# Weighing the exponentials of a sparse attention inside their transposes: one diagonal product in place of a scaling and a transpose

## The chip, the cores and the metric

One Trainium2 chip, one of its cores. The time is the device time of one execution in microseconds, as the median of a kernel's runs. The core's engines are TensorE (PE in the profile, its weight loads apart as PEld), VectorE (DVE), ScalarE (ACT), GpSimd (POOL) and SyncE (SP), each with an instruction queue of its own; they wait for one another through semaphores.

## What is computed

A network of three layers runs on 256 tokens of width 1024: a first layer (latent attention beside a recurrence, then experts), an even layer and an odd layer, each of the last two with a feed-forward part. The change lies in the odd layer's attention, which for 8 pairs of heads has a compressed branch, a "selected" branch and a window branch. With 256 tokens all blocks are selected and the window covers everything, so both of the latter are causal attentions over all keys, each with its own keys and values, and each weighed by a gate of its own per token and head:

```
s = jnp.einsum('bqghd,bgqnld->bqghnl', qb, kg).astype(jnp.float32) * scale
p = safe_softmax(s.reshape(B, C_Q_BLOCK, C_GROUPS, C_HPG, top_n * SEL_BLOCK), m_slc)
o_slc = jnp.einsum('bqghnl,bgqnld->bqghd', p.astype(vg.dtype), vg)
...
s = jnp.einsum('bqghd,bsgd->bqghs', qb, kwb).astype(jnp.float32) * scale
p = safe_softmax(s, m_win)
o_win = jnp.einsum('bqghs,bsgd->bqghd', p.astype(vwb.dtype), vwb)
g = qslice(gates, i, C_Q_BLOCK)
return g[..., 0:1] * o_cmp + g[..., 1:2] * o_slc + g[..., 2:3] * o_win
```

So each row of exponentials is multiplied by gate / sum before it meets the values.

## The kernel before

The kernel is a sequence of stages with a barrier between them. The function of the change, `sparse_attention`, is one stage; before it `odd_in` makes queries, keys and values, after it `out_ffn` multiplies by the output matrix and runs the feed-forward part. Each stage has hand-written programs for each engine, and the order of the work on an engine is the order of its code; there is no scheduler.

`sparse_attention` runs over 16 units (`units`). Unit u is a pair of heads n and a branch b, `n, b = divmod(u, 2)`; i counts the two heads of the pair. The 256 query tokens are two tiles of 128 (t); by causality tile 0 sees 128 keys and tile 1 sees 256 (`SPAN`), so a head has 384 columns (`NCOL`) of exponentials, in three blocks of 128x128.

A unit goes through these steps, by the names in the code:

- `score(u)` (TensorE, L3596 and L3601): mask and scores into `pS`, signal `scored`.
- `smallest(u)` (VectorE, L3511): the row extremes `low_max`, signal `least`.
- `exps(u)` (ScalarE, L3472): four exponentials into `E`, with row sums into `den`, signal `exped`. From u = 2 on it first waits until unit u-2 has been turned (`probs_turned`), since `E` has two buffers.
- `weigh(u)` (VectorE, L3519 to L3525): gate over sum into `part`, then the four pieces of `E` are multiplied in place, signal `weighed`.
- `turn(u)` (TensorE, L3613): six transposes of 128x128 from `E` into `pT`, signal `probs_turned`. It waits for `weighed`, and for the copies of the unit before, as `pT` has one buffer.
- `left(u)` and `right(u)` (VectorE L3532, ScalarE L3481): copies of `pT` into `ET`.
- `add_values(u)` (TensorE, L3626; for b = 1 also the compressed branch, L3634): products with the values into `pO`; after every second unit `high(n)` (ScalarE, L3485) and `rest(n)` (VectorE, L3536) take the result out as two f16 parts, `mixT`.

The engines' programs interleave units. In iteration u, TensorE does `score(u+2)`, `turn(u)`, `add_values(u-1)`; ScalarE does `exps(u+2)`, in odd iterations `high`, then `right(u)`; VectorE does `smallest(u+2)`, `weigh(u+1)`, `left(u)`, and in odd iterations `rest`. TensorE also does the 16 compressed scores (L3643) before iteration 0 and four transposes for them (L3658) in iteration 2. `Link` makes VectorE wait for its own previous result.

Of the kernel before, what the change touches and what calls it, by code (L numbers as in the profile page):

```python
# [9 lines left out]
ALU = mybir.AluOpType  # L10
# [7 lines left out]
P = 128  # L18
SEQ = 256
TT = SEQ // P  # L20
# [13 lines left out]
SPAN = [(0, 0, P), (1, P, SEQ)]  # L34
# [1689 lines left out]
def first_mix(nc, con, m, out, low, shifted, x, wt, w, ring, views, slots, expert, h, scratch, keep, start):  # L1724
# [9 lines left out]
    with ExitStack() as ctx:  # L1734
# [3 lines left out]
        probs = turned4[:].rearrange("p u n -> p (u n)")  # L1738
        E = probs[:, 0:4 * NCOL].rearrange("p (s i n) -> p s i n", s=2, i=2)
        ET = probs[:, 4 * NCOL:8 * NCOL].rearrange("p (s i n) -> p s i n", s=2, i=2)  # L1740
        low_max = sb("low_max", [P, 2, TT, 2])
# [59 lines left out]
        with Stage(nc, "rw", RW_NAMES + TAIL_NAMES + ["few_" + n for n in FEW_NAMES] + ["moe_" + n for n in MOE_NAMES]) as sems:  # L1801
# [33 lines left out]
            with nc.Block(no_gpsimd_drain=True) as block:  # L1835
# [62 lines left out]
                def _(pe):  # L1898
# [131 lines left out]
                    def turn_probs(u):  # L2030
# [5 lines left out]
                        for i in range(2):  # L2036
                            for n in range(3):
                                ins = T.transpose(pB[:, P_BANK[i], n * P:(n + 1) * P], E[:, u % 2, i, n * P:(n + 1) * P],
                                                  con["identity"])
# [187 lines left out]
                def _(act):  # L2227
                    copy = lambda o, i, scale=1.0: nc.scalar.activation(o, i, ACT.Copy, scale=scale)

                    def exps_of(u):  # L2230
# [5 lines left out]
                        for i in range(2):  # L2236
                            for t, c0, nk in SPAN:
                                ins = nc.scalar.activation(E[:, at, i, c0:c0 + nk], scores(u)[:, i, c0:c0 + nk], ACT.Exp,
                                                           bias=low_max[:, at, t, i:i + 1], scale=m.nrq[:, 0, t, 2 * u + i:2 * u + i + 1],
# [732 lines left out]
def even_attention(nc, con, y, e, low, outT, start):  # L2972

    units = 8
    with ExitStack() as ctx:
# [3 lines left out]
        part = sb("part", [P, 2, 2, TT])  # L2979
        E = sb("E", [P, 2, 2, NCOL])  # L2980
        ET = sb("ET", [P, 2, 2, NCOL])
        st = sb("st", [P, 3, 8])
# [444 lines left out]
def sparse_attention(nc, con, y, o, low, outT, start):  # L3427
# [4 lines left out]
    with ExitStack() as ctx:  # L3432
        sb = lambda n, s, d=F32: ctx.enter_context(nc.sbuf_tensor(f"nsa_{n}", s, d))
# [2 lines left out]
        den = sb("den", [P, 2, 2, TT])  # L3436
        part = sb("part", [P, 2, 2, TT])
        E = sb("E", [P, 2, 2, NCOL])
        ET = sb("ET", [P, 2, 2, NCOL])
        cS = sb("cS", [P, 2, TT, PAIRS, CMP_KEYS])  # L3440
        c_max = sb("c_max", [P, n_cmp])
# [4 lines left out]
        pT = ctx.enter_context(nc.psum_tensor("nsa_pT", [P, 2, 512], F32))  # L3446
# [5 lines left out]
        with Stage(nc, "nsa", ["scored", "least", "exped", "weighed", "probs_turned",  # L3452
# [4 lines left out]
            with nc.Block(no_gpsimd_drain=True) as block:  # L3457
# [44 lines left out]
                @block.vector  # L3502
                def _(dve):
                    link = Link(dve, vlink)

                    def smallest(u):
                        dve.wait_ge(scored, u + 1)
                        if u >= 2:
                            dve.wait_ge(exped, u - 1)
                        for t, c0, nk in SPAN:  # L3510
                            ins = nc.vector.tensor_reduce(low_max[:, u % 2, :, t], pS[:, u % 2, :, c0:c0 + nk], AX_X,  # L3511
                                                          ALU.min)
                        ins.then_inc(least, 1)

                    def weigh(u):
                        dve.wait_ge(exped, u + 1)
                        n, b = divmod(u, 2)
                        at = u % 2
                        link(nc.vector.tensor_tensor(part[:, at], den[:, at], gate[:, b + 1, 2 * n:2 * n + 2, :],  # L3519
                                                     ALU.mult))  # L3520
                        link(nc.vector.reciprocal(part[:, at], part[:, at]))
                        for i in range(2):
                            for t, c0, nk in SPAN:
                                into = E[:, at, i, c0:c0 + nk]
                                ins = nc.vector.tensor_scalar(into, into, part[:, at, i, t:t + 1], None, ALU.mult)  # L3525
                        ins.then_inc(weighed, 1)

                    def left(u):
                        dve.wait_ge(probs_turned, u + 1)
                        if u >= 2:  # L3530
                            dve.wait_ge(summed, u - 1)
                        nc.vector.tensor_copy(ET[:, u % 2, 0, :], pT[:, 0, 0:NCOL]).then_inc(probs_left, 1)  # L3532

                    def rest(n):
                        dve.wait_ge(high_out, n + 1)
                        nc.vector.tensor_tensor(outT[1][:, n, :], pO[:, n % 2, 0:SEQ], outT[0][:, n, :],  # L3536
                                                ALU.subtract).then_inc(low_out, 1)

                    over = lambda v: v.unsqueeze(2).broadcast_to([P, n_cmp, CMP_KEYS])
                    flat = cS[:].rearrange("p i t n k -> p (i t n) k")  # L3540

                    def compressed_scores():
                        dve.wait_ge(c_scored, 1)
                        for i in range(2):
                            mask = con["cmp_mask"].rearrange("p (t k) -> p t k", t=TT).unsqueeze(2)\
                                .broadcast_to([P, TT, PAIRS, CMP_KEYS])
                            ins = nc.vector.tensor_tensor(
                                cS[:, i], pT[:, 0, :].rearrange("p (t n i k) -> p i t n k", t=TT, i=2, k=CMP_KEYS)[:, i], mask,
                                ALU.add)
                            link(ins)  # L3550
                        dve.sem_inc(c_masked, 1)
                        link(nc.vector.tensor_reduce(c_max[:], flat, AX_X, ALU.min))
                        nc.vector.tensor_tensor(flat, flat, over(c_max[:]), ALU.subtract).then_inc(c_less, 1)

                    def compressed_weights():
                        dve.wait_ge(c_exped, 1)
                        link(nc.vector.tensor_reduce(c_den[:], flat, AX_X, ALU.add))
                        as_heads = c_den[:].rearrange("p (i t n) -> p i t n", i=2, t=TT)
                        link(nc.vector.tensor_tensor(c_part[:], as_heads, gate_cmp, ALU.mult))
                        link(nc.vector.reciprocal(c_part[:], c_part[:]))  # L3560
                        nc.vector.tensor_tensor(flat, flat, over(c_part[:].rearrange("p i t n -> p (i t n)")),
                                                ALU.mult).then_inc(c_weighed, 1)

                    dve.wait_ge(gate_exps, 1)
                    link(nc.vector.tensor_scalar(gates[:], gates[:], 1.0, None, ALU.add))
                    smallest(0)
                    smallest(1)
                    weigh(0)
                    for u in range(units):
                        if u == 0:  # L3570
                            compressed_scores()
                        if u + 2 < units:
                            smallest(u + 2)
                        if u == 2:
                            dve.wait_ge(c_turned, 1)
                            nc.vector.tensor_copy(cT[:].rearrange("p i s -> p (i s)"), pO[:, 1, :]).then_inc(c_out, 1)
                        if u + 1 < units:
                            weigh(u + 1)
                        left(u)
                        if u == 1:  # L3580
                            compressed_weights()
                        if u >= 3 and u % 2:
                            rest((u - 3) // 2)
                    rest(PAIRS - 1)

                @block.tensor
                def _(pe):
                    ident = con["identity"]
# [17 lines left out]
                    def turn(u):  # L3606
                        pe.wait_ge(weighed, u + 1)
                        if u > 0:
                            pe.wait_ge(probs_left, u)
                            pe.wait_ge(probs_right, u)  # L3610
                        for i in range(2):
                            for k, (t, kb, at) in enumerate(blocks):
                                ins = nc.tensor.transpose(pT[:, i, k * P:(k + 1) * P], E[:, u % 2, i, at:at + P], ident)  # L3613
                        ins.then_inc(probs_turned, 1)

                    def add_values(u):
# [23 lines left out]
                    for n in range(PAIRS):  # L3640
                        for t in range(TT):
                            at = (t * PAIRS + n) * 2 * CMP_KEYS
                            ins = nc.tensor.matmul(pT[:, 0, at:at + 2 * CMP_KEYS], qT[:, n, t * P:(t + 1) * P],  # L3643
                                                   kcT[:, n // per_group].rearrange("p i k -> p (i k)"), start=True, stop=True,
                                                   skip_group_check=True)
                    ins.then_inc(c_scored, 1)
                    for u in range(units):
# [5 lines left out]
                        if u == 2:  # L3653
                            pe.wait_ge(c_weighed, 1)
                            for i in range(2):
                                for t in range(TT):
                                    at = i * SEQ + t * P
                                    ins = nc.tensor.transpose(pO[:, 1, at:at + P], cS[:, i, t].rearrange("p n k -> p (n k)"), ident)  # L3658
# [126 lines left out]
```

## Time and profile before

| | before |
|---|---|
| median of 3 runs | 1140.2 us (1139.49 to 1145.4) |
| profiled execution, span from first to last instruction | 1135.1 us |
| TensorE busy | 998.4 us (88%) |
| VectorE busy | 590.4 us (52%) |
| ScalarE busy | 486.3 us (43%) |
| `sparse_attention`, first score to last result | 853.3 to 921.0 us |

The profile gives no total of its own for the profiled execution: its span of 1135.1 us is 5.1 us less than the median of the runs, and changes of the span are set against it. In the timeline, "idle before" is in brackets with the instruction that ended the wait; several instructions of one kind are one row with their count, and the time of such a row is from the first's start to the last's end. An f32 product can have more records in the trace than the program has instructions; the counts of both are given where this matters.

### The profile page before, as it was taken

To read this page: it belongs to the slowest core of one execution; us is meant where nothing else is said; L and a number is where in the kernel's file an instruction comes from. 1 tells how busy PE (TensorE), PEld (TensorE's weight loads), DVE (VectorE), ACT (ScalarE), POOL (GpSimd) and SP (SyncE) were. 2 spreads that over 40 slices of the span, in tenths; PEclk is the share of its full clock that TensorE was granted. 3 is DMA by queue.
4 is the path that set the end of the run, shared out by engine and by line. 5 is a ranking of instruction groups with operands and counts; after the bars stand their busy time and mean duration, and the time that the engine had idled before them with its cause. 6 is when DMAs were issued, how large, how long until landed. Compare 5 with 4: busy or idle time off the path is not lost. (4 is left out here: it accounts for less than half of the span.)

```text
span 1135.1 us, 20168 instructions
## 1 busy us (share of the span) xinstructions
PE 998.4 (88%) x8497; PEld 710.3 (63%) x8499; DVE 590.4 (52%) x950; ACT 486.3 (43%) x795; POOL 101.3 (9%) x111
## 2 busy tenths in 40 slices
PE   6998899799666677998799999997998879999996
PEld 5675787455333344886547777775885536777773
DVE  5566589421000004688666555435667865555543
ACT  5456452310000004545556455524545656645532
POOL 3410360000000001033000000002040000000000
PEclk9899899799888898998889999998998999999999
DMA  9822005999999996452094755525422046666520
GB/s 273 247 90 82 2 3 226 422 409 420 421 421 421 421 411 195 155 177 76 1 329 133 243 193 184 183 105 153 149 82 75 1 174 216 223 222 204 188 89 37
DMA packets 108324, 228.56 MB, mean 201 GB/s; under 512 B 7145, under 2 KB 86043, under 8 KB 93659
## 3 DMA queue, kind: packets, MB, share of 16 engines
q1 hardware_dynamic: 105275, 219.38, 53.2%
q0 software_dynamic: 2976, 8.14, 2.5%
q8 instruction: 53, 0.87, 0.3%
q14 instruction: 20, 0.16, 0.0%
HBM read 224.63 MB, written 1.05 MB: 199 GB/s over the span
## 5 line engine op out<-in xcount | busy, mean ns | idle before, releaser
L524 DVE SCALAR_TENSOR_TENSOR ffn_wu_lo<-ffn_w_up,ffn_wu_hi 128x2048 f16<-128x2048 f32 x44 | 99.0, 2288 | 55.2 <-ACT ffn_wu_hi L449 55.2
L1132 PE MATMUL rw_pB<-ring,kept 128*32 128x256 f32 x864 | 69.2, 418 | 31.4 <-DMA ring<-in_w_up 22.0
L669 PE MATMUL ffn_pG<-ffn_hT_hi,ffn_wu_hi 128*128 128x256 f16 x352 | 96.0, 273 | 0.3
L669 PE MATMUL ffn_pG<-ffn_hT_lo,ffn_wu_hi 128*128 128x256 f16 x352 | 96.0, 273 | 0.0
L669 PE MATMUL ffn_pG<-ffn_hT_hi,ffn_wu_lo 128*128 128x256 f16 x352 | 96.0, 273 | 0.0
L669 PE MATMUL ffn_pU<-ffn_hT_hi,ffn_wu_hi 128*128 128x256 f16 x352 | 95.9, 273 | 0.0
L669 PE MATMUL ffn_pU<-ffn_hT_hi,ffn_wu_lo 128*128 128x256 f16 x352 | 95.9, 273 | 0.0
L669 PE MATMUL ffn_pU<-ffn_hT_lo,ffn_wu_hi 128*128 128x256 f16 x352 | 95.9, 273 | 0.0
L449 ACT ACTIVATE ffn_wu_hi<-ffn_w_up 128x2048 f16<-128x2048 f32 x44 | 81.7, 1901 | 2.5 <-DMA ffn_w_up<-in_ffn_w_gate 2.3
L1132 PEld LDWEIGHTS rw_pB<-ring,kept 128*32 128x32 f32 x864 | 37.9, 120 | 59.9 <-issue 46.6
L249 DVE SCALAR_TENSOR_TENSOR in_w_lo<-wt,in_w_hi 128x2048 f16<-128x2048 f32 (+2 forms) x22 | 52.7, 2396 | 35.7 <-ACT in_w_hi L242 35.2
L1065 DVE TENSOR_TENSOR rw_mu_a<-rw_pB,rw_mu_a 128x256 f32<-128x256 f32 x8 | 3.4, 424 | 125.7 <-PE rw_pB L1132 125.7
L542 DVE SCALAR_TENSOR_TENSOR ffn_hidden<-ffn_pU,ffn_gated 128x512 f32<-128x512 f32 x22 | 15.2, 690 | 90.4 <-ACT ffn_gated L463 90.4
L524 DVE SCALAR_TENSOR_TENSOR ffn_wd_lo<-ffn_w_down,ffn_wd_hi 128x2048 f16<-128x2048 f32 x22 | 50.4, 2291 | 22.1 <-ACT ffn_wd_hi L449 22.1
L678 PE MATMUL ffn_pY<-ffn_wd_hi,ffn_h_hi 128*128 128x512 f16 x176 | 53.6, 379 | 0.6 <-DVE ffn_h_lo L524 0.6
L678 PE MATMUL ffn_pY<-ffn_wd_lo,ffn_h_hi 128*128 128x512 f16 x176 | 53.7, 379 | 0.0
L678 PE MATMUL ffn_pY<-ffn_wd_hi,ffn_h_lo 128*128 128x512 f16 x176 | 53.7, 379 | 0.0
L463 ACT ACTIVATE ffn_gated<-ffn_pG 128x512 f32<-128x512 f32 x22 | 13.1, 597 | 93.2 <-PE ffn_pU L669 93.0
L336 PE MATMUL in_pY<-in_w_hi,in_sT_hi 128*128 128x256 f16 (+2 forms) x352 | 45.8, 279 | 0.4
L1153 PE MATMUL rw_pB<-ring,rw_mu_a 128*32 128x512 f32 x240 | 34.4, 679 | 11.2 <-DMA ring<-in_w_down 7.9
L242 ACT ACTIVATE in_w_hi<-wt 128x2048 f16<-128x2048 f32 (+2 forms) x22 | 42.2, 1917 | 4.2 <-DMA wt<-in_od_w_in 2.4
L336 PE MATMUL in_pY<-in_w_hi,in_sT_lo 128*128 128x256 f16 (+2 forms) x352 | 43.0, 276 | 0.0
(651 smaller groups left out, 2129.1 us busy)
## 6 DMA issues: line engine op xcount, KB each, us to landing
ring<-in_w_gate SPq DMA_DIRECT2D x27, 1024.0 KB, 26.1
ring<-in_w_up SPq DMA_DIRECT2D x27, 1024.0 KB, 26.4
ring<-in_w_down SPq DMA_DIRECT2D x26, 1024.0 KB, 26.6
ffn_w_up<-in_ffn_w_gate SPq DMA_DIRECT2D x22, 1024.0 KB, 7.6
ffn_w_up<-in_ffn_w_up SPq DMA_DIRECT2D x22, 1024.0 KB, 9.8
ffn_w_down<-in_ffn_w_down SPq DMA_DIRECT2D x22, 1024.0 KB, 5.1
wt<-in_ev_w_in SPq DMA_DIRECT2D x9, 1024.0 KB, 5.6
wt<-in_od_w_in SPq DMA_DIRECT2D x9, 1024.0 KB, 6.4
```

Source lines behind the costliest of these rows:

```text
L242: self.nc.scalar.activation(self.w_hi[:, k % 2, :, 0:n], self.wt[:, k % 2, :, 0:n], ACT.Copy, scale=W_SCALE).then_inc(self.hi_ready, 1)
L249: self.nc.vector.scalar_tensor_tensor(self.w_lo[:, k % 2, :, 0:n], self.wt[:, k % 2, :, 0:n], W_SCALE, self.w_hi[:, k % 2, :, 0:n], ALU.mu ...
L336: ins = self.nc.tensor.matmul(self.pY[:, slot, t, 0:n], x[:, c, t * P:(t + 1) * P], w[:, slot, c, 0:n], start=(term == 0 and c == 0), stop ...
L449: copy = lambda o, i, scale=1.0: nc.scalar.activation(o, i, ACT.Copy, scale=scale)
L463: nc.scalar.activation(gated[:, s, :], pG[:, s, :], ACT.Silu, scale=1.0 / W_SCALE).then_inc(silu_done, 1)
L524: return nc.vector.scalar_tensor_tensor(out, whole, scale, hi, ALU.mult, ALU.subtract)
L542: nc.vector.scalar_tensor_tensor(into, pU[:, s, :], 1.0 / W_SCALE, gated[:, s, :], ALU.mult, ALU.mult).then_inc(hidden_ready, 1)
L669: ins = T.matmul(p[:, s, j * SEQ:(j + 1) * SEQ], w[:, s, m, c, j::NJ], h[:, c, :], start=(n == 0), stop=(n == 3 * KC - 1))
L678: return T.matmul(pY[:, t, half * 512:(half + 1) * 512], h[:, s, at:at + P], w[:, s, j, half * 512:(half + 1) * 512], start=False, stop=st ...
L1065: nc.vector.tensor_tensor(hidden[:], pU[:, 0:D_EXPERT], gated[:], ALU.mult).then_inc(hidden_ready, 1)
L1132: ins = nc.tensor.matmul(into[i * CAP:(i + 1) * CAP, 0:D_EXPERT], h[:, c, i * CAP:(i + 1) * CAP], held[:, c * D_EXPERT:(c + 1) * D_EXPERT] ...
L1153: ins = nc.tensor.matmul(pD[i * CAP:(i + 1) * CAP, half, :], hidT[:, j, i * CAP:(i + 1) * CAP], held[:, at:at + 512], start=(j == 0), stop ...
```

## The change

`E` stays as ScalarE wrote it. `weigh(u)` now writes, with one VectorE operation, four 128x128 diagonal matrices (head i, tile t): the identity times `part` of each row, 128x512 elements in all, into a new double-buffered tile `scale`. `turn(u)` multiplies each block of `E` by the diagonal matrix of its head and tile: the product of the transposed block with the diagonal is the transposed and weighed block. The loops, the waits, the signals and the other steps stay.

```diff
@@ tiles
         E = sb("E", [P, 2, 2, NCOL])
+        scale = sb("scale", [P, 2, 2 * TT, P])
         ET = sb("ET", [P, 2, 2, NCOL])
@@ weigh(u), VectorE
                         link(nc.vector.reciprocal(part[:, at], part[:, at]))
-                        for i in range(2):
-                            for t, c0, nk in SPAN:
-                                into = E[:, at, i, c0:c0 + nk]
-                                ins = nc.vector.tensor_scalar(into, into, part[:, at, i, t:t + 1], None, ALU.mult)
-                        ins.then_inc(weighed, 1)
+                        each = part[:, at].rearrange("p i t -> p (i t)").unsqueeze(2).broadcast_to([P, 2 * TT, P])
+                        ones = con["identity"].unsqueeze(1).broadcast_to([P, 2 * TT, P])
+                        nc.vector.tensor_tensor(scale[:, at], ones, each, ALU.mult).then_inc(weighed, 1)
@@ turn(u), TensorE
-                                ins = nc.tensor.transpose(pT[:, i, k * P:(k + 1) * P], E[:, u % 2, i, at:at + P], ident)
+                                ins = nc.tensor.matmul(pT[:, i, k * P:(k + 1) * P], E[:, u % 2, i, at:at + P], scale[:, u % 2, i * TT + t, :],
+                                                       start=True, stop=True, skip_group_check=True)
```

On VectorE, iteration 0 of the stage before the change (`nsa_E` is the tile `E`, `nsa_part` the factors, `nsa_ET` the copies of the turned blocks):

```order
L3511 TENSOR_REDUCE nsa_low_max<-nsa_pS 128x2 x2
L3519 TENSOR_TENSOR nsa_part<-nsa_den,od_gates 128x4
L3521 RECIPROCAL nsa_part<-nsa_part 128x4
L3525 TENSOR_SCALAR nsa_E<-nsa_E,nsa_part 128x128
L3525 TENSOR_SCALAR nsa_E<-nsa_E,nsa_part 128x256
L3525 TENSOR_SCALAR nsa_E<-nsa_E,nsa_part 128x128
L3525 TENSOR_SCALAR nsa_E<-nsa_E,nsa_part 128x256
L3532 COPY nsa_ET<-nsa_pT 128x384
```

And with the change:

```order
L3512 TENSOR_REDUCE nsa_low_max<-nsa_pS 128x2 x2
L3520 TENSOR_TENSOR nsa_part<-nsa_den,od_gates 128x4
L3522 RECIPROCAL nsa_part<-nsa_part 128x4
L3525 TENSOR_TENSOR nsa_scale<-con_identity,nsa_part 128x512
L3531 COPY nsa_ET<-nsa_pT 128x384
```

Four operations became one; nothing moved past another.

On TensorE, iteration 3 before (the scores of unit 5, the turn of unit 3, the values of unit 2):

```order
L3596 MATMUL nsa_pS<-low 128x2x128 x2
L3601 MATMUL nsa_pS<-od_kT,od_qT 128x128 x2
L3601 MATMUL nsa_pS<-od_kT,od_qT 128x256 x2
L3613 MATMUL nsa_pT<-con_identity,nsa_E 128x128 x6
L3626 MATMUL nsa_pO<-nsa_ET,y_odd 64x256 x2
L3626 MATMUL nsa_pO<-nsa_ET,y_odd 64x128 x2
```

And with the change:

```order
L3595 MATMUL nsa_pS<-low 128x2x128 x2
L3600 MATMUL nsa_pS<-od_kT,od_qT 128x128 x2
L3600 MATMUL nsa_pS<-od_kT,od_qT 128x256 x2
L3612 MATMUL nsa_pT<-nsa_scale,nsa_E 128x128 x6
L3626 MATMUL nsa_pO<-nsa_ET,y_odd 64x256 x2
L3626 MATMUL nsa_pO<-nsa_ET,y_odd 64x128 x2
```

The six instructions of a turn stand where they stood, with `nsa_scale` in the place of the identity, and as ordinary products.

## Rows read from the trace of the kernel before

**Rows 1.** The page: span.

```profile
span 1135.1 us, 20168 instructions
```

**Rows 2.** Waits from 856 to 920 us: who waited for whom, total, times, longest.

```profile
ACT nsa_E L3472 <- DVE nsa_low_max L3511: 23.8, 16, 4.8
```

**Rows 3.** Timeline of one round of two units: start, length, engine, line, idle before.

```profile
879.36 0.85 PE L3613 MATMUL nsa_pT<-con_identity,nsa_E 128*128 128x128 f32 x6 [0.83 <-ACT nsa_ET L3481]
...
880.29 0.37 ACT L3472 ACTIVATE nsa_E<-nsa_pS,nsa_low_max 128x128 f32<-128x128 f32 x1 [1.08 <-DVE nsa_low_max L3511]
...
881.89 0.50 ACT L3481 ACTIVATE nsa_ET<-nsa_pT 128x384 f32<-128x384 f32 x1
...
882.55 0.87 PE L3613 MATMUL nsa_pT<-con_identity,nsa_E 128*128 128x128 f32 x6
882.67 1.02 DVE L3511 TENSOR_REDUCE nsa_low_max<-nsa_pS 128x2 f32<-128x256 f32 x2 [0.66 <-PE nsa_pS L3601]
...
883.35 0.87 PE L3626 MATMUL nsa_pO<-nsa_ET,y_odd 128*64 128x256 f32 x8
...
883.72 0.37 ACT L3472 ACTIVATE nsa_E<-nsa_pS,nsa_low_max 128x128 f32<-128x128 f32 x1 [1.33 <-DVE nsa_low_max L3511]
...
884.01 1.01 DVE L3525 TENSOR_SCALAR nsa_E<-nsa_E,nsa_part 128x128 f32<-128x128 f32 x4
...
885.58 0.51 ACT L3481 ACTIVATE nsa_ET<-nsa_pT 128x384 f32<-128x384 f32 x1
...
886.24 0.85 PE L3613 MATMUL nsa_pT<-con_identity,nsa_E 128*128 128x128 f32 x6 [0.83 <-ACT nsa_ET L3481]
```

**Rows 4.** Timeline of the stage's first units.

```profile
863.31 1.54 PE L3613 MATMUL nsa_pT<-con_identity,nsa_E 128*128 128x128 f32 x6
...
864.94 0.37 ACT L3472 ACTIVATE nsa_E<-nsa_pS,nsa_low_max 128x128 f32<-128x128 f32 x1 [4.84 <-DVE nsa_low_max L3511]
...
867.18 0.86 PE L3613 MATMUL nsa_pT<-con_identity,nsa_E 128*128 128x128 f32 x6 [0.33 <-ACT nsa_ET L3481]
...
868.13 0.37 ACT L3472 ACTIVATE nsa_E<-nsa_pS,nsa_low_max 128x128 f32<-128x128 f32 x1 [0.58 <-DVE nsa_low_max L3511]
...
870.37 0.84 PE L3613 MATMUL nsa_pT<-con_identity,nsa_E 128*128 128x128 f32 x6 [0.35 <-ACT nsa_ET L3481]
...
871.73 0.66 PE L3658 MATMUL nsa_pO<-con_identity,nsa_cS 128*128 128x128 f32 x4 [0.51 <-DVE nsa_cS L3561]
...
875.67 0.88 PE L3613 MATMUL nsa_pT<-con_identity,nsa_E 128*128 128x128 f32 x6
...
876.84 0.37 ACT L3472 ACTIVATE nsa_E<-nsa_pS,nsa_low_max 128x128 f32<-128x128 f32 x1 [2.11 <-DVE nsa_low_max L3511]
```

**Rows 5.** Timeline of its last two turns.

```profile
913.75 0.85 PE L3613 MATMUL nsa_pT<-con_identity,nsa_E 128*128 128x128 f32 x6 [2.01 <-ACT nsa_ET L3481]
...
916.43 1.54 PE L3613 MATMUL nsa_pT<-con_identity,nsa_E 128*128 128x128 f32 x6
```

**Rows 6.** TensorE, f32 records: two groups by line, and another stage's timeline.

```profile
L3613 PE MATMUL nsa_pT<-con_identity,nsa_E 128*128 128x128 f32 x96 | 15.1, 298 | 6.9 <-ACT nsa_ET L3481 6.9
...
L3643 PE MATMUL nsa_pT<-od_kcT,od_qT 128*128 128x32 f32 x32 | 4.2, 292 | 0.0
...
180.43 2.00 PE L1992 MATMUL rw_pB<-ring 128*128 128x128 f32 x16
182.27 0.95 PE L1999 MATMUL rw_pB<-ring 128*128 128x64 f32 x7
```

**Rows 7.** VectorE group: line, shape, count, busy us and mean ns, idle.

```profile
L3561 DVE TENSOR_TENSOR nsa_cS<-nsa_cS,nsa_c_part 128x512 f32<-128x512 f32 x1 | 0.7, 691 | 0.0
```

**Rows 8.** Windows: length, busy of PE, PEld, DVE, ACT, POOL, then granted clock.

```profile
863.00:864.00 1.00, 1.00 (x5) 0.69 (x4) 0.96 (x3) 0.00 (x0) 0.00 (x0) 0.50 0.00 0
...
915.00:916.00 1.00, 1.00 (x10) 0.66 (x6) 0.47 (x2) 0.12 (x1) 0.00 (x0) 0.51 0.00 0
```

**Rows 9.** The chain that ended last, in order of time, after the stage.

```profile
952.39 5.40 PE ffn_pG L669 x48
```

## The prediction

> **What bounds the kernel now.** First the page: the span is 1135.1 us [rows 1], of which the changed stage takes 68 us, from 853.3 to 921.0 us. After it the feed-forward part follows a barrier and is TensorE's alone: 48 products run in 5.40 us from 952.39 us on, and so the chain goes on, group after group [rows 9]. Nothing there waits for something that an earlier start could have fetched, so a microsecond more or less in the attention is one at the end of the kernel.
>
> Then the waits inside the stage. The longest item is ScalarE waiting for the row extremes, 23.8 us in 16 waits [rows 2]. That tells where ScalarE idles, not what the loop is. For this I read the timeline of one round of two units, which repeats every 886.24 - 879.36 = 6.88 us [rows 3]. The reader is to see one closed loop in it. Call the even unit E and the odd one O. `turn(E)` starts on TensorE at 879.36. TensorE then works without a gap worth naming through `add_values`, the scores of unit O+2, and reaches `turn(O)` at 882.55. The end of those scores releases `smallest(O+2)` on VectorE at 882.67, which takes 1.02 us and releases `exps(O+2)` on ScalarE at 883.72. ScalarE's queue then has `high` and `right(O)`, at 885.58 for 0.51 us. Its end, 886.09, releases the next even turn at 886.24, after TensorE stood idle for 0.83 us. So the loop runs TensorE, VectorE's reduction, ScalarE, and back.
>
> VectorE's weighing is in none of these steps. It is at 884.01 for 1.01 us [rows 3], ends at 885.02, and the turn that needs it starts at 886.24, 1.2 us later.
>
> **The change on VectorE.** The four scalings of a unit take 1.01 us together [rows 3]. The one operation in their place has 128x512 elements, all in SBUF, one operand broadcast along the row. The nearest row has just that shape and form and takes 691 ns [rows 7]. So a weighing gets 0.32 us shorter, 5.1 us over 16 units. By the slack of 1.2 us this is worth nothing at the end, and with the work that hides it gone it could be worth those 5.1 us at most. Bounds for the new operation: from nothing to twice the row, 1.4 us, which is 0.4 us more than now and still inside the slack.
>
> **The change on TensorE.** The six transposes of a turn leave 96 records for 96 instructions [rows 6]. They take 883.35 - 882.55 = 0.80 us from the turn's start to the next group's start [rows 3]. An ordinary f32 product is different: the 16 products of the compressed scores leave 32 records [rows 6]. Their form has only 32 columns, so for the time of one record I take another stage's products of 128x128 by 128 columns: 16 records from 180.43 to the next group's start at 182.27, 0.115 us each with the loads of their weights inside [rows 6]. Six diagonal products are then 12 records. The six more cost d = 6 x 0.115 = 0.69 us a turn at the full clock. Bounds for d: nothing, if a diagonal product should cost what a transpose costs, and 2.07 us, which I price among the rivals. I take 0.69, since that row has exactly the new product's shape.
>
> **What d does in a round.** `turn(E)` is in the loop, so the scores of O+2 end d later, and `smallest(O+2)` with them: +0.69 us. `turn(O)` was not in the loop: `exps(O+2)` also has to wait until unit O has been turned, since it overwrites its `E`, but that turn ended at 882.55 + 0.87 = 883.42, 0.30 us before the exponentials started. With d in both turns it ends at 883.42 + 0.69 + 0.69 = 884.80 and now is the later of the two releases; with the 0.03 us that ScalarE needs to react the exponentials start at 884.83 in place of 883.72. So a round gets 1.11 us longer, or 2d - 0.27 for other d. The checks on the other side: `exps(E+2)` started at 880.29 and now waits for `turn(E)`, 879.36 + 0.85 + 0.69 = 880.90, so `right(E)`, which began at 881.89 and took 0.50, ends near 883.0 and releases `turn(O)` near 883.15; TensorE comes there at 882.55 + 0.69 = 883.24. That is still in time, by 0.1 us. There are five rounds from the turn of unit 4 to that of unit 14 (879.36 to 913.75, [rows 3, 5]): 5 x 1.11 = 5.55 us.
>
> **The start.** There TensorE's granted clock is 0.50, its level of 1.2 GHz [rows 8], and the first turn takes 1.54 us [rows 4] for 0.87 at the full level. The six more records cost twice 0.115 each there, 1.3 us. The exponentials of unit 2 waited for this turn (863.31 + 1.54 = 864.85, they start at 864.94), so they and the turn of unit 1 come 1.25 us later. That turn, with its own 0.69, ends at 867.18 + 0.86 + 1.25 + 0.69 = 869.98, and the exponentials of unit 3, before at 868.13, start at 870.01: +1.88. So does the turn of unit 2 (870.37). Its 0.69 is partly absorbed, as the four compressed transposes behind it waited 0.51 us for VectorE; they start near 873.74, before 871.73: +2.0. The turn of unit 3 (875.67, 0.88 long) ends at 875.67 + 0.88 + 2.0 + 0.69 = 879.24, the exponentials of unit 5, before at 876.84, start at 879.27: +2.4 us [rows 4].
>
> **The end.** The last two turns (913.75 and 916.43) cost d each, 1.38 us. The second stood in a stretch at 0.51 [rows 8], after TensorE had idled 2.01 us, and took 1.54 in place of 0.87 us [rows 5]; that cost 0.67 us in this turn and, by my estimate, as much again in the products around it, 1.3 us. With more work on TensorE the idle before it is some 0.2 us shorter. If the full level holds, 1.38 - 1.3 = 0.1 us remain; if it falls as before, the second turn's six records cost 1.38 and both together 2.0 us. I take the first.
>
> **Sum:** 2.4 + 5.55 + 0.1 = 8.0 us, a span of 1143.1, and a median of 1140.2 + 8.0 = 1148.2 us, 0.7% slower.
>
> **A rule on the clock.** The diagonal products stand where transposes stood. In the trace, the clock stayed at 0.50 through the stretch that holds the first turn's transposes, with TensorE busy all the time [rows 8]. The Trainium skill, TensorE: Matmul & The Clock Gate, section "Part 4: PE-mode transpose", says that a transpose does not count as TensorE being busy in the way a product does. By that rule the products would bring the full clock back earlier in the start. This is the clock rival below.
>
> **The rivals.**
>
> *The clock comes back early.* If the level rises near 864.2 us, inside the first turn, six to eight records of the first turn and the scores behind it run at the full level. The first turn then ends near 865.3, only 0.45 us later than before; with 0.69 for the second turn, the start costs 1.55 in place of 2.4 us, the sum is 7.1, the time 1147.3 us. For it: a busy TensorE at a low clock that transposes may explain. Against: scores run in the same stretch and did not raise it. Chance 0.15.
>
> *Only the even turns count.* If ScalarE's release by `turn(O)` has slack that I don't see, each of the six stretches loses 0.69 and not 1.11: 8.0 - 6 x 0.42 = 5.5 us, 1145.7 us. Against it stands the wait in the code and the 0.30 us of slack in [rows 3]. Chance 0.08.
>
> *The clock falls at the end, or once more in a round:* 8.0 + 1.9 = 9.9 us, 1150.1 us. For it: the long wait before the last even turn stays. Chance 0.25.
>
> *A product costs four transposes.* Then a turn has the time of 24 records, 2.76 us, d = 2.07, a round 2 x 2.07 - 0.27 = 3.87 more, the five rounds 19, start and end 13 more: about 1172 us. Against it: two records for a product, each as long as a transpose's [rows 6]. Chance 0.03. The Trainium skill, the same page, section "Terms", calls the transpose mode four times faster for FP32; the sum by it would be this one, and the rows here bear out a factor of two.
>
> *Not slower.* A diagonal product passes as one record, at a transpose's price. Nothing in the loop changes, VectorE's 0.32 us lie in slack, and the time is 1140.2, or a few tenths less. Between this and my forecast the sum moves by about 14.5 us for each microsecond of d (two for each of five rounds, 4.5 for start and end), so the kernel is slower by less than 5.7 us for d under 0.53, that is for added records of less than 0.09 us. For it: only the flag of the instruction and its operand differ. Against it: the compressed scores' 32 records. Chance 0.06.
>
> The forecast has the remaining 0.43.
>
> **How the numbers follow.** 0.5% of the time, 5.7 us, is about what a measurement of this kernel can tell from no change. The likeliest case gives 1148.2. The forecast, both clock cases and most of "only the even turns" make up 0.9 between 1145.7 and 1150.1; the ends get half a microsecond to one and a half more, as the runs before scatter by 1 us around their median and more to the slow side: 1145.2 to 1151.5. Slower: the forecast, the clock cases, four transposes, and half of the even turns, less something for the scatter, 0.86. Same: 0.13. Faster: nothing that I found gives 5.7 us, since VectorE's whole saving is 5.1, 0.01.
>
> **What would show it right or wrong.** `turn` has 192 records, a turn takes about 1.5 us, the weighing one operation of about 0.69 us; a round takes about 8.0 us; `exps(O+2)` is released by `turn(O)` and not by the extremes; VectorE's and ScalarE's idle times grow. Wrong would be: 96 records, or a record far from 0.115 us; a round of 6.88; a half-clock stretch in the middle rounds; or a weighing well over 1.4 us, which would bring VectorE into the loop.

## The result

| | before | changed |
|---|---|---|
| median of 15 runs each | 1139.76 us (1129.64 to 1145.4) | 1147.35 us (1142.13 to 1156.58) |
| ratio to before | | 1.0087, 95% interval 1.0063 to 1.0111 |
| span of the profiled execution | 1135.1 us | 1143.2 us |

The kernel became 0.9% slower by the ratio, about 10 us; the two medians lie 7.6 us apart. The ratios here and below leave out executions over 1.5% above the fastest of their kernel and the medians don't, so the two can differ. The forecast was 1148.2 us, in a range of 1145.2 to 1151.5.

First the page of the changed kernel: its span and busy times.

```profile
span 1143.2 us, 20314 instructions
PE 1006.3 (88%) x8595; PEld 722.6 (63%) x8595; DVE 585.8 (51%) x902; ACT 486.0 (43%) x795; POOL 98.6 (9%) x111
```

VectorE has 48 instructions less (902, before 950) and is busy for 4.6 us less. TensorE has 98 records more, 96 of them in the turns, and is busy for 7.9 us more. Next the records of the changed instructions, by source line: number, then shortest, median and longest in ns, and where the first and the last of them start.

```profile
L3612 PEld LDWEIGHTS nsa_pT<-nsa_scale,nsa_E x192: 186/192/333, 862.8 to 926.0; 128*128 128x128 f32 x192
L3612 PE MATMUL nsa_pT<-nsa_scale,nsa_E x192: 275/275/580, 862.8 to 926.1; 128*128 128x128 f32 x192
L3525 DVE TENSOR_TENSOR nsa_scale<-con_identity,nsa_part x16: 691/692/693, 855.3 to 922.3; 128x512 f32<-128x512 f32 x16
```

So 96 products leave 192 records, where 96 transposes left 96 [rows 6], and the one VectorE operation takes 692 ns, where its model row had 691 [rows 7]. Now one round of the timeline, the counterpart of [rows 3]:

```profile
881.43 1.58 PE L3612 MATMUL nsa_pT<-nsa_scale,nsa_E 128*128 128x128 f32 x12 [0.62 <-ACT nsa_ET L3482]
...
883.09 0.37 ACT L3473 ACTIVATE nsa_E<-nsa_pS,nsa_low_max 128x128 f32<-128x128 f32 x1 [1.81 <-DVE nsa_low_max L3512]
...
885.35 1.60 PE L3612 MATMUL nsa_pT<-nsa_scale,nsa_E 128*128 128x128 f32 x12
885.46 1.02 DVE L3512 TENSOR_REDUCE nsa_low_max<-nsa_pS 128x2 f32<-128x256 f32 x2 [1.70 <-PE nsa_pS L3600]
...
886.88 0.87 PE L3626 MATMUL nsa_pO<-nsa_ET,y_odd 128*64 128x256 f32 x8
887.04 0.37 ACT L3473 ACTIVATE nsa_E<-nsa_pS,nsa_low_max 128x128 f32<-128x128 f32 x1 [1.85 <-DVE nsa_low_max L3512]
...
888.90 0.51 ACT L3482 ACTIVATE nsa_ET<-nsa_pT 128x384 f32<-128x384 f32 x1
...
889.55 1.58 PE L3612 MATMUL nsa_pT<-nsa_scale,nsa_E 128*128 128x128 f32 x12 [0.62 <-ACT nsa_ET L3482]
```

The reader is to see three things. First, the odd turn now takes 886.88 - 885.35 = 1.53 us to the next group's start, where it took 0.80. So d, the forecast's name for what the six added records of a turn cost, is 0.73. Second, the exponentials of unit O+2 start 887.04 - 885.35 = 1.69 us after the odd turn's start; before it was 883.72 - 882.55 = 1.17. Third, the round is 889.55 - 881.43 = 8.12 us long (8.13 from turn to turn over five rounds), before 6.88. The bracket at 887.04 names the extremes as what ended ScalarE's wait. They ended at 885.46 + 1.02 = 886.48, which is 0.56 us too early for that; the odd turn ended at 886.95. Experiment e7 settles which it was.

Then the stage's first turn and its last two, for [rows 4] and [rows 5]:

```profile
862.84 2.93 PE L3612 MATMUL nsa_pT<-nsa_scale,nsa_E 128*128 128x128 f32 x12
...
922.06 1.58 PE L3612 MATMUL nsa_pT<-nsa_scale,nsa_E 128*128 128x128 f32 x12 [1.80 <-ACT nsa_ET L3482]
...
924.80 1.60 PE L3612 MATMUL nsa_pT<-nsa_scale,nsa_E 128*128 128x128 f32 x12
...
928.41 0.38 ACT L3486 ACTIVATE mixT_hi<-nsa_pO 128x256 f16<-128x256 f32 x1 [1.48 <-PE nsa_pO L3634]
```

The last row is the last copy of ScalarE's `high`. Before the change it was this one:

```profile
920.14 0.38 ACT L3485 ACTIVATE mixT_hi<-nsa_pO 128x256 f16<-128x256 f32 x1 [1.64 <-PE nsa_pO L3634]
```

From the first turn's start to the turn of unit 4 it is 881.43 - 862.84 = 18.59 us, before 879.36 - 863.31 = 16.05. To the last even turn it is 40.63 us, before 34.39. The last two turns run at the full clock.

That makes 2.5 + 6.2 us up to the last even turn. From there to the last copy it is 6.39 us before (913.75 to 920.14) and 6.35 us now (922.06 to 928.41). And from that copy to the end of the span it is 215.0 us before and 214.8 us now (214 to 216 us in the experiments): what the attention lost came through to the end of the kernel, as the forecast's first step had it. The sum, 8.7 us, stands beside a span that grew by 8.1 us. The two don't have to agree: ahead of the first turn the two executions differ in ways that the change doesn't touch, most of it shown in the last section.

### The profile page after: what moved, and what is told of

Same layout as the page of the kernel before. It is cut to its first block and busy times, and to the rows that moved or that the text cites. A ratio compares the mean times of both kernels' runs of the same rounds, so it can differ in the third digit from the quotient of the medians.

```text
span 1143.2 us, 20314 instructions
## 1 busy us (share of the span) xinstructions
PE 1006.3 (88%) x8595; PEld 722.6 (63%) x8595; DVE 585.8 (51%) x902; ACT 486.0 (43%) x795; POOL 98.6 (9%) x111
## 5 line engine op out<-in xcount | busy, mean ns | idle before, releaser
L336 PE MATMUL in_pY<-in_w_lo,in_sT_hi 128*128 128x256 f16 (+2 forms) x352 | 42.2, 273 | 0.0
```

The source lines that it names most:

```text
L336: ins = self.nc.tensor.matmul(self.pY[:, slot, t, 0:n], x[:, c, t * P:(t + 1) * P], w[:, slot, c, 0:n], start=(term == 0 and c == 0), stop ...
```

## Experiments

The measure for most is the round, the time from one even turn to the next. It repeated to 0.02 us between executions of the same kernel, while whole executions of one kernel lie up to 1 or 2% apart. Of e5, e6 and e9 there is one execution each, so they have a round and no ratio. Each edit is against the kernel before (e1, e3, e8) or the changed one (e2, e5, e6, e7, e9); in the longer ones only the changed lines are shown.

**e1, TensorE's part alone.**

```diff
-ins = nc.tensor.transpose(pT[:, i, k * P:(k + 1) * P], E[:, u % 2, i, at:at + P], ident)
+ins = nc.tensor.matmul(pT[:, i, k * P:(k + 1) * P], E[:, u % 2, i, at:at + P], ident,
+                       start=True, stop=True, skip_group_check=True)
```

> The kernel before, with only the turns changed: six ordinary f32 products with the identity in place of six transposes; VectorE still scales the exponentials in place. Theory (two turns in the loop): the turns' extra 12 records per round are all that costs, and VectorE's saving is worth nothing; so the round from the turn of unit 4 to that of unit 6 is that of the changed kernel, 8.13 us (before: 6.88), and the ratio to the kernel before is 1.007 to 1.011. Rival (VectorE's part matters): with the old scalings VectorE has 0.64 us more to do per round, and the round is longer than 8.13, up to 8.8; or, if the broadcast operation itself does harm to the others, shorter than 8.13.

Two consecutive even turns in its timeline:

```profile
903.10 1.58 PE L3613 MATMUL nsa_pT<-con_identity,nsa_E 128*128 128x128 f32 x12 [0.63 <-ACT nsa_ET L3481]
...
911.23 1.58 PE L3613 MATMUL nsa_pT<-con_identity,nsa_E 128*128 128x128 f32 x12 [0.63 <-ACT nsa_ET L3481]
```

The round is 8.13 us, the changed kernel's, though VectorE still does the four scalings. The medians are 1148.58 against 1140.88 us, but the ratio, 1.0029 (0.9989 to 1.0069), lies under the expected 1.007 to 1.011 and its interval ends just short of it: a miss for the ratio. The round decides: its whole growth is in the turns.

**e2, VectorE's part alone.**

```diff
-ins = nc.tensor.matmul(pT[:, i, k * P:(k + 1) * P], E[:, u % 2, i, at:at + P], scale[:, u % 2, i * TT + t, :],
-                       start=True, stop=True, skip_group_check=True)
+ins = nc.tensor.transpose(pT[:, i, k * P:(k + 1) * P], E[:, u % 2, i, at:at + P], ident)
```

> The changed kernel with only VectorE's part: the diagonals are written, but the turns are transposes with the identity, so the exponentials go into the values unweighed (the weighing is left out of the result). Theory: a round of 6.88 us as before, ratio 1.000 within its interval, since weighing is off the loop by 1.2 us. Rival (VectorE's saving counts): the round falls by up to 0.64 us to 6.24, and the ratio to 0.995 or less. Rival (the new operation does harm): a round above 6.9.

```profile
905.60 0.85 PE L3612 MATMUL nsa_pT<-con_identity,nsa_E 128*128 128x128 f32 x6 [0.84 <-ACT nsa_ET L3482]
...
912.48 0.85 PE L3612 MATMUL nsa_pT<-con_identity,nsa_E 128*128 128x128 f32 x6 [0.83 <-ACT nsa_ET L3482]
```

The round is 6.88 us, the ratio 1.0004 (0.9962 to 1.0046). The 0.64 us a round that VectorE saves buys nothing there.

Outside the rounds it does buy something, once. In the start, the transposes of the compressed branch wait for VectorE:

```profile
877.32 0.66 PE L3657 MATMUL nsa_pO<-con_identity,nsa_cS 128*128 128x128 f32 x4 [0.20 <-DVE nsa_cS L3560]
```

Before they waited 0.51 us [rows 4], here 0.20. From the first turn to the turn of unit 4 it is 15.73 us (869.22 to 884.95), 0.32 less than before, which is what one weighing got shorter. With products in the turns this gain is not seen: from the turn of unit 2 to that of unit 3 it takes 5.21 us in the changed kernel (872.01 to 877.22), and just as long in e1 with its scalings.

**e3, twelve records of transposes.**

```diff
-ins = nc.tensor.transpose(pT[:, i, k * P:(k + 1) * P], E[:, u % 2, i, at:at + P], ident)
+for _ in range(2):
+    ins = nc.tensor.transpose(pT[:, i, k * P:(k + 1) * P], E[:, u % 2, i, at:at + P], ident)
```

> The kernel before, with each of the six transposes of a turn issued twice into the same place, 12 records a turn. Theory (records count, whatever their kind): a turn takes what 12 product records take, within 0.05 us, the round is 8.0 to 8.15 us, the ratio 1.007 to 1.011. Rival (the kind matters for the clock): the granted clock inside the stage is lower or stays at 0.5 longer than in the changed kernel, as transposes are not seen as work, and the time is 1 to 3 us longer than the changed kernel's. Rival (a product's weight load costs more than a transpose's): rounds 0.2 us or more shorter than 8.13.

Four rows of its timeline, an even turn, the odd one, the next even one, and the turn of unit 14:

```profile
897.82 1.50 PE L3614 MATMUL nsa_pT<-con_identity,nsa_E 128*128 128x128 f32 x12 [0.62 <-ACT nsa_ET L3481]
901.66 1.53 PE L3614 MATMUL nsa_pT<-con_identity,nsa_E 128*128 128x128 f32 x12
905.80 1.50 PE L3614 MATMUL nsa_pT<-con_identity,nsa_E 128*128 128x128 f32 x12 [0.62 <-ACT nsa_ET L3481]
...
921.76 2.65 PE L3614 MATMUL nsa_pT<-con_identity,nsa_E 128*128 128x128 f32 x12 [1.80 <-ACT nsa_ET L3481]
```

And its weight loads, from the records by line, to be set against the changed kernel's 186/192/333 ns:

```profile
L3614 PEld LDWEIGHTS nsa_pT<-con_identity,nsa_E x192: 137/141/230, 863.6 to 927.2; 128*128 128x128 f32 x192
```

The round is 7.98 us, just under the expected 8.0 to 8.15, and the ratio 1.0058 (1.001 to 1.0105), under the expected one but with an interval that holds most of it. An odd turn takes 1.53 us from its first record's start to its last one's end, with six transposes it took 0.87 [rows 3] and with six products 1.60. So six more transposes cost 0.66 us, and products cost 0.07 us a turn beyond that. The number of records is nine tenths of the price. The rival on weight loads asked for 0.2 us a round and got 0.15. A product's weight load is 51 ns longer in the median, but that this is where the 0.07 us come from is not shown; the kind of the record is part of the truth, and small. As to the clock, the turn of unit 14 stood at the low level here (2.65 us), and in the changed kernel at the full one (1.58 us). This is taken up in the last section.

**e4, the changed kernel again.** No edit.

> The changed kernel once more, to see what repeats of its profile: 8.13 us a round and 0.73 us more a turn should repeat to 0.02 us; the place and length of the half-clock stretch at the stage's start should not, and should move the stage's length by 1 to 4 us. Ratio 1.006 to 1.011.

The round is 8.13 us, the ratio 1.0078 (1.0042 to 1.0114). From the first turn to the turn of unit 4 it is 18.36 us (18.59 the first time). From the start of the stage to that first turn, though, it is 866.62 - 858.99 = 7.6 us, where the first execution took 862.84 - 849.64 = 13.2 us. That is 5.6 us, more than the 1 to 4 us expected. Another difference is inside the first turn:

```profile
866.62 2.69 PE L3612 MATMUL nsa_pT<-nsa_scale,nsa_E 128*128 128x128 f32 x12
```

It takes 2.69 us where the first execution took 2.93. The windows of e4 have the granted clock at 0.50 from 866 to 868 us, at 0.54 from 868 to 869 and at 1.00 behind that, so the full level came back just before the turn ended.

**e5 and e6, products in the even or in the odd units only.** The edit is that of e5; e6 has `u % 2 == 1`.

```diff
@@ weigh(u)
+if u % 2 == 0:
     nc.vector.tensor_tensor(scale[:, at], ones, each, ALU.mult).then_inc(weighed, 1)
+else:
+    for i in range(2):
+        for t, c0, nk in SPAN:
+            into = E[:, at, i, c0:c0 + nk]
+            ins = nc.vector.tensor_scalar(into, into, part[:, at, i, t:t + 1], None, ALU.mult)
+    ins.then_inc(weighed, 1)
@@ turn(u)
+if u % 2 == 0:
     ins = nc.tensor.matmul(pT[:, i, k * P:(k + 1) * P], E[:, u % 2, i, at:at + P], scale[:, u % 2, i * TT + t, :],
                            start=True, stop=True, skip_group_check=True)
+else:
+    ins = nc.tensor.transpose(pT[:, i, k * P:(k + 1) * P], E[:, u % 2, i, at:at + P], ident)
```

> Even units by diagonals and products as in the changed kernel, odd units by scalings and transposes as before. Theory: the even turn lies in the loop with its whole price, and the odd one keeps its slack of 0.3 us before the exponentials, so the round is 6.88 + 0.73 = 7.61 us. Rival (each turn costs its half of the 1.25 us): 7.50 us. Rival (only the sum of TensorE's work counts, any idle of it is used): near 7.2.

> Odd units by diagonals and products, even units by scalings and transposes. Theory: the odd turn delays only the exponentials that overwrite its buffer, by its 0.73 us less the slack, so the round is 6.88 + 0.52 = 7.40 us, and the exponentials behind it are released by the turn. Rival (each turn costs its half): 7.50 us. Rival (odd turns do not count): 6.88 us.

Of e5 two even turns:

```profile
887.20 1.58 PE L3620 MATMUL nsa_pT<-nsa_scale,nsa_E 128*128 128x128 f32 x12 [0.83 <-ACT nsa_ET L3482]
...
894.81 1.58 PE L3620 MATMUL nsa_pT<-nsa_scale,nsa_E 128*128 128x128 f32 x12 [0.83 <-ACT nsa_ET L3482]
```

And of e6:

```profile
888.83 0.84 PE L3623 MATMUL nsa_pT<-con_identity,nsa_E 128*128 128x128 f32 x6 [0.62 <-ACT nsa_ET L3482]
...
896.23 0.85 PE L3623 MATMUL nsa_pT<-con_identity,nsa_E 128*128 128x128 f32 x6 [0.62 <-ACT nsa_ET L3482]
```

The rounds are 7.61 and 7.40 us, both as the theory had them. (In e6 the trace names the extremes and not the turn as the release of the exponentials behind the odd turn; e7 shows what such a name is worth.) The even turn counts with all of its 0.73 us and the odd one with 0.52. TensorE's idle time before the even turn tells the two apart as well: it stays at 0.83 us with even products, since all that TensorE adds there passes through, and falls to 0.62 with odd ones.

**e7, three buffers for the exponentials.**

```diff
-E = sb("E", [P, 2, 2, NCOL])
-scale = sb("scale", [P, 2, 2 * TT, P])
+E = sb("E", [P, 3, 2, NCOL])
+scale = sb("scale", [P, 3, 2 * TT, P])
@@ exps(u)
 if u >= 2:
-    act.wait_ge(probs_turned, u - 1)
     act.wait_ge(weighed, u - 1)
+if u >= 3:
+    act.wait_ge(probs_turned, u - 2)
```

`E` and `scale` are indexed by `u % 3` in place of `u % 2` wherever they stand.

> The changed kernel with three buffers for the exponentials and the diagonals, so that the exponentials of unit u wait for the turn of unit u-3 and no longer for that of u-2. Theory: the odd turn leaves the loop, its 0.52 us a round come back, the round is 7.61 us and the ratio to the kernel before 1.003 to 1.008. Rival (the exponentials are held by the extremes, as the profile of the changed kernel names them as the releaser): the round stays at 8.13 us.

An odd turn, the exponentials behind it, and the two even turns around:

```profile
886.48 1.58 PE L3613 MATMUL nsa_pT<-nsa_scale,nsa_E 128*128 128x128 f32 x12
...
890.40 1.60 PE L3613 MATMUL nsa_pT<-nsa_scale,nsa_E 128*128 128x128 f32 x12
...
891.58 0.37 ACT L3474 ACTIVATE nsa_E<-nsa_pS,nsa_low_max 128x128 f32<-128x128 f32 x1 [2.00 <-DVE nsa_low_max L3513]
...
894.10 1.58 PE L3613 MATMUL nsa_pT<-nsa_scale,nsa_E 128*128 128x128 f32 x12
```

The exponentials start 1.18 us after the odd turn's start, as before the change, and the round is 7.62 us, 0.51 less. So the release in the changed kernel was the odd turn, and the name in its bracket was wrong. The ratio, 1.0011 (0.9973 to 1.0049), lies below the expected 1.003 to 1.008 with an interval that holds only its lower part.

**e8, the kernel before in another order.**

```diff
@@ ScalarE, iteration u
+right(u)
 if u + 2 < units:
     exps(u + 2)
 if u >= 3 and u % 2:
     high((u - 3) // 2)
-right(u)
@@ VectorE, iteration u, and after the last
-if u >= 3 and u % 2:
-    rest((u - 3) // 2)
+if u >= 4 and u % 2 == 0:
+    rest((u - 4) // 2)
+rest(PAIRS - 2)
 rest(PAIRS - 1)
```

> The kernel before, with ScalarE's copy of a turned unit ahead of the next exponentials in its queue, and VectorE's rest() moved half a round later, so that it does not hold the reduction behind it. Theory (the loop closes through ScalarE's queue): the even turn no longer waits for exponentials and high, the round falls from 6.88 to about 6.3 us, and the ratio is 0.995 to 0.998. Rival (the exponentials, now behind the copy, are late by 0.3 us or more and take it all back): 6.9 us or more.

Two even turns and the weight loads of the second, with VectorE's weighing of its unit and the copy behind it:

```profile
878.58 0.85 PE L3614 MATMUL nsa_pT<-con_identity,nsa_E 128*128 128x128 f32 x6
...
883.23 1.01 DVE L3525 TENSOR_SCALAR nsa_E<-nsa_E,nsa_part 128x128 f32<-128x128 f32 x4
884.15 0.55 DVE L3532 COPY nsa_ET<-nsa_pT 128x384 f32<-128x384 f32 x1
...
884.77 0.64 PEld L3614 LDWEIGHTS nsa_pT<-con_identity,nsa_E 128*128 128x128 f32 x6 [0.55 <-DVE nsa_E L3525]
884.80 0.84 PE L3614 MATMUL nsa_pT<-con_identity,nsa_E 128*128 128x128 f32 x6 [0.18 <-issue]
```

The round is 6.22 us, the ratio 0.9988 (0.995 to 1.0026), just above the expected one. The even turn no longer waits for ScalarE: the loop did close through its queue, and the copies of a turned unit were at its wrong end. (The edit moves `rest` too; the share of each is not shown.) The bracket now names the weighing (`nsa_E`), but that ended at 884.24, 0.53 us before the weight load. What ended just before it, at 884.70, is VectorE's copy of the turned unit, for which the turn also waits. In VectorE's queue that copy stands right behind the weighing, so the weighing, which had 1.2 us of slack before, is now on the path, though TensorE stands idle for it only 0.18 us a round.

**e9, VectorE's new operation twice.**

```diff
+link(nc.vector.tensor_tensor(scale[:, at], ones, each, ALU.mult))
 nc.vector.tensor_tensor(scale[:, at], ones, each, ALU.mult).then_inc(weighed, 1)
```

> The changed kernel, with VectorE writing each unit's diagonals twice, one after the other: 0.7 to 0.8 us more per unit on VectorE. Theory (VectorE has slack in the round): the round stays at 8.13 us within 0.05. Rival (VectorE's time is passed on to the loop): 8.9 to 9.6 us a round.

```profile
885.45 1.57 PE L3613 MATMUL nsa_pT<-nsa_scale,nsa_E 128*128 128x128 f32 x12 [0.62 <-ACT nsa_ET L3482]
...
893.58 1.58 PE L3613 MATMUL nsa_pT<-nsa_scale,nsa_E 128*128 128x128 f32 x12 [0.62 <-ACT nsa_ET L3482]
```

8.13 us: a weighing of 1.4 us costs no more than one of 0.69.

**e10, the changed kernel in the order of e8.** The edit of e8 is made to the changed kernel.

> The changed kernel with the order of e8 (copies of a turned unit ahead of the next exponentials, rest() half a round later). Theory: the loop through ScalarE is gone and TensorE is the bound with its work of one round, 8.13 less the 0.62 us that it idled, 7.5 us; ratio to the kernel before 1.003 to 1.007. Rival (in this order VectorE's shorter weighing pays, as the turn waited for it in e8): 6.9 us or less, at or below the kernel before.

```profile
907.06 1.60 PE L3613 MATMUL nsa_pT<-nsa_scale,nsa_E 128*128 128x128 f32 x12
...
914.53 1.60 PE L3613 MATMUL nsa_pT<-nsa_scale,nsa_E 128*128 128x128 f32 x12
```

The round is 7.47 us, no turn in the rounds waits any more, and TensorE's own work is the bound. The ratio is 1.0024 (0.999 to 1.0058), a little under the expected 1.003 to 1.007. Even where the weighing is on the path without the change, the products cost more than they save: 7.47 against 6.22 us.

**e11, e8 again.** No edit.

> e8 once more with more rounds, to settle its ratio: a round of 6.22 us, 0.66 us less than before, makes 3.3 us in five rounds and about 4 us in all, so a ratio of 0.9965 is expected; 1.000 or more would mean that the start or the end of the stage gives it back.

The round is 6.22 us again (900.54 to 906.77). The ratio is 0.9962 (0.9929 to 0.9994), with e8's 0.9988 (0.995 to 1.0026) before it. The order of e8 without the diagonals is the fastest version here, by about 0.4% by the second measurement; the first alone doesn't tell it from no change. The start takes some of the gain back: from the first turn to the turn of unit 4 it is 16.85 us in e8 and 16.55 in e11, before 16.05.

The rounds side by side:

| kernel | even turn | odd turn | round, us |
|---|---|---|---|
| before, e2 | transposes | transposes | 6.88 |
| e6 | transposes | products | 7.40 |
| e5 | products | transposes | 7.61 |
| e7 (three buffers) | products | products | 7.62 |
| e3 | 12 transposes | 12 transposes | 7.98 |
| changed, e1, e4, e9 | products | products | 8.13 |
| e8, e11 (other order) | transposes | transposes | 6.22 |
| e10 (other order) | products | products | 7.47 |

## Why the prediction was right

**VectorE's saving is worth nothing.** Shown for the rounds: e2 takes the weighing alone and keeps 6.88 us, e9 doubles the operation and keeps 8.13. The operation's 692 ns were those of its model row. In the start e2 gains 0.32 us once, where the compressed transposes wait for VectorE; the forecast did not look for that, and with products in the turns it does not show.

**A product leaves two records, at 0.115 us each.** The count is shown by the 192 records. The price was mis-sized by a little: 0.73 us a turn in place of 0.69. By e3, the records' number makes 0.66 of it and their kind 0.07. I had taken one rate and multiplied it by the six added records; the kind applies to all twelve.

**2d - 0.27 a round.** The form is shown by e5 (d in the even turn in full, 7.61), e6 (the odd turn less the slack, 7.40) and e7 (with a third buffer the odd part is gone, 7.62). Its value was 1.25 us, forecast 1.11. Of the difference, 0.08 is d. The rest, 0.06, is the slack: ScalarE starts 0.09 us after the odd turn's modelled end (886.95 to 887.04) and not 0.03. A row of the forecast had this already: the exponentials of unit 2 started at 864.94, 0.09 us after the turn that released them ended at 863.31 + 1.54 = 864.85 [rows 4]. Five rounds made 6.24 us in place of 5.55.

**The start, 2.4 us.** Measured from the first turn to the turn of unit 4, 2.54 and 2.31 us in the two executions. The first turn became 2.93 us long, from 1.54; 1.3 was forecast for the six more records at the low clock, and 1.39 came in the first execution and 1.15 in e4.

**The end, 0.1 us.** Measured -0.04: two turns of products, at the full clock. That the clock would hold was a choice of mine and not argued from a row that could decide it, so that this term came out is luck. The low stretch was priced at 1.3 us. By the runs it is about 1.5: in e3, with its low stretch at the end, it is 929.58 - 921.76 = 7.82 us from the last even turn to the last copy, and 6.35 us in the changed kernel with turns of nearly the same length.

```profile
929.58 0.38 ACT L3485 ACTIVATE mixT_hi<-nsa_pO 128x256 f16<-128x256 f32 x1 [1.48 <-PE nsa_pO L3635]
```

**The sum.** 2.3 to 2.5, 6.2 and -0.04 make 8.5 to 8.7 us from the first turn on, 8.0 were forecast. The ratio says about 10 with an interval from 7 to 13, and the medians 7.6. That the span came out at 1143.2 for a forecast of 1143.1 is luck: the stage began 3.7 us earlier in this execution (849.64, before 853.34), and the way to its first turn took 3.2 us longer (13.2, before 10.0), neither of which the change touches, and the two nearly cancel.

**The rivals.** "Only the even turns" falls by e6. "Four transposes" and "not slower" fall by the 192 records; the factor between a turn of products and one of transposes is 1.53 / 0.80 = 1.9. "The clock falls at the end" did not occur in any execution of the changed kernel that was profiled. Of the clock rival, the early return in the start, part is seen. In the first execution the low level lasted through the first turn (2.93 us), but in e4, e1, e5 and e9 it ended inside a first turn of products, which took 2.69, 2.42, 2.65 and 2.58 us. In e4 that made the start 0.2 us shorter, where the rival had 0.85. Whether the products bring the level back is open: the low stretches also began at different times.

Wrong was one of the signs that I named: the profile was to show the odd turn as the release of the exponentials. It does so once, for the exponentials of unit 5, and names the extremes in every round after that, though e7 shows that the turn was the release. The statement about the kernel was right and the statement about its trace was not.

## What to carry to other kernels

To fold a scaling into an f32 transpose makes it an f32 product with two records for one: here 1.46 us more of TensorE's work a round cost 1.25 us, and 0.64 us less of VectorE's gave nothing back, since its weighing was not in the loop. Before such a trade, follow the round once around and ask of every engine how late it could be, and of each added piece of work which release it will overtake, here that of the buffer which the odd turn frees with 0.2 us to spare. If a wait's named releaser had ended half a microsecond earlier, as in the changed kernel and in e8, look in the code for the other semaphore of the same wait.

## What the runs showed of the hardware

The compressed scores stand before the first turn, and no kernel here changes them. They took three different times. Here is their row in the changed kernel's timeline, and behind it that of e4, which is the same code:

```profile
853.87 7.03 PE L3643 MATMUL nsa_pT<-od_kcT,od_qT 128*128 128x32 f32 x32
```

```profile
861.34 3.76 PE L3643 MATMUL nsa_pT<-od_kcT,od_qT 128*128 128x32 f32 x32
```

Before they took 4.16 us. Over 13 executions it was 7.03 us in seven, about 4.2 in three and 3.76 in three. The windows of the changed kernel show a granted clock of 0.50 over all of it:

```profile
853.00:857.00 4.00, 4.00 (x21) 3.35 (x17) 1.96 (x5) 3.42 (x16) 0.00 (x0) 0.50 0.84 343
857.00:861.00 4.00, 4.00 (x21) 3.84 (x20) 0.06 (x1) 0.00 (x0) 0.00 (x0) 0.50 0.00 0
```

In e4 the window from 862 to 866 us, which holds most of that row, shows 0.94. So the same stretch of the same kernel can run at 1.2 or at 2.4 GHz, here a matter of 3.3 us, and one profile before and one after can differ by this alone. What sets it is not shown. A round inside the stage, in all these traces at the full level, repeats to 0.02 us and is the better measure.

At the stage's end TensorE idles for 1.8 to 2.0 us before the last even turn. With transposes in all turns (before, e2, e3) a low stretch followed in all three executions: the turn of unit 15 took 1.54 us in before and e2, and that of unit 14 took 2.65 us in e3. With products in all, the even or the odd turns (changed, e1, e4, e9; e5; e6) the level stayed full in all six. In e6 the turn right behind the idle of 1.80 us is one of transposes, as in e3, and only the turns ahead of it and behind it are products:

```profile
918.43 0.85 PE L3623 MATMUL nsa_pT<-con_identity,nsa_E 128*128 128x128 f32 x6 [1.80 <-ACT nsa_ET L3482]
...
920.44 1.60 PE L3620 MATMUL nsa_pT<-nsa_scale,nsa_E 128*128 128x128 f32 x12
```

In e8 and e11 the level stayed full with transposes, after an idle of only 1.36 us. This agrees with what the Trainium skill says in TensorE: Matmul & The Clock Gate, section "Part 4: PE-mode transpose", that a transpose does not count as TensorE being busy in the way a product does. It is an agreement in nine executions and not shown as the cause, as no experiment here isolates it. Should it be the cause, the products gave back about 1.5 us at the end, the price of the low stretch in e3, of what they cost elsewhere.
